# A compressed branch's first layer with high and low weights as one moving operand of 512 columns, and its parts added in the turn

## The reference

```python
blk = kr[:, idx] + pos[None, None, :, None, :]          # 31 windows of 32 tokens
flat = blk.transpose(0, 1, 3, 2, 4).reshape(B, nc, G, CMP_BLOCK * D)
return jax.nn.gelu(flat @ w1 + b1) @ w2                 # (62 x 2048) @ (2048 x 256)
```

## Time and profile before

| what | before |
|---|---|
| median of 3 runs | 1667.31 us (1667.16 to 1668.07) |
| profiled execution, its own time | 1668.98 us |
| its span | 1667.2 us |
| what lies around the span | 1.8 us |
| granted TensorE clock, mean | 0.996 of 2.4 GHz |
| TensorE busy | 1635.2 us, 98% |
| VectorE, ScalarE, GpSimd busy | 42%, 41%, 45% |

### The profile page before, as it was taken

How to read it: one execution, slowest core, us unless ns; L and a number is a source line. 1 busy time by engine, 2 the same in 40 slices (tenths; PEclk the granted TensorE clock), 3 DMA queues, 4 the chain that set the end, 5 groups by cost and what they waited for, 6 DMA issues and landing times.

```text
span 1667.2 us, 21229 instructions
## 1 busy us (share of the span) xinstructions
PE 1635.2 (98%) x8088; PEld 1349.0 (81%) x8088; DVE 692.5 (42%) x1395; ACT 684.6 (41%) x1204; POOL 753.7 (45%) x574
## 2 busy tenths in 40 slices
PE   9999999999999999999999999999999999999997
PEld 7777778888888887888888888888778888888885
DVE  6176664884444226312212225555673311112224
ACT  5366655543334324422223234566573422223322
POOL 7424325574445552744444553543113554444550
PEclk9999999999999999999999999999999999999999
DMA  5411102232232231323223222212002232222231
GB/s 202 146 51 51 39 14 101 102 101 91 99 102 90 99 101 51 123 93 101 97 92 101 95 96 101 89 65 77 26 26 89 89 101 95 95 101 92 98 101 51
DMA packets 42117, 147.37 MB, mean 88 GB/s; under 512 B 4768, under 2 KB 5152, under 8 KB 42016
## 3 DMA queue, kind: packets, MB, share of 16 engines
q1 hardware_dynamic: 40536, 143.13, 25.4%
q10 hardware_dynamic: 1480, 2.89, 0.5%
HBM read 142.84 MB, written 3.41 MB: 88 GB/s over the span
## 4 chain that ended last, share of the span: by engine, by line
PE 91%; DVE 3%; ACT 3%; issue 2%; DMA 1%; POOL 1%; DVEq 0%; ACTq 0%; POOLq 0%
PE PS L492 20%; PE PS L493 20%; PE PS L494 20%; PE PS L1059 5%; PE PS L1070 5%; PE PS L467 4%; PE PS L891 4%; PE PS L867 3%; PE PS L474 2%; PE PS L882 2%; PE PS L514 1%; PE PS L516 1%; PE PS L515 1%; DVE L L975 1%; POOL w_lo L536 0%
## 5 line engine op out<-in xcount | busy, mean ns | idle before, releaser
L536 POOL TENSOR_TENSOR w_lo<-stage,w_hi 128x512 fp32r<-128x512 f32 x524 | 709.5, 1379 | 843.5 <-ACT w_hi L524 842.5
L524 ACT ACTIVATE w_hi<-stage 128x1024 fp32r<-128x1024 f32 x262 | 274.7, 1057 | 509.1 <-DMA stage<-in_weights 508.9
L492 PE MATMUL PS<-H_hi,w_hi 128*128 128x512 f32 x992 | 387.7, 391 | 0.4 <-DVE rcol L1249 0.4
L494 PE MATMUL PS<-H_hi,w_lo 128*128 128x512 f32 x992 | 385.9, 389 | 0.0
L493 PE MATMUL PS<-H_lo,w_hi 128*128 128x512 f32 x992 | 385.9, 389 | 0.0
L492 PEld LDWEIGHTS PS<-H_hi,w_hi 128*128 128x128 f32 x992 | 186.2, 188 | 40.3 <-issue 1.0
L493 PEld LDWEIGHTS PS<-H_lo,w_hi 128*128 128x128 f32 x992 | 186.2, 188 | 39.5 <-issue 1.0
L494 PEld LDWEIGHTS PS<-H_hi,w_lo 128*128 128x128 f32 x992 | 186.2, 188 | 38.6
L492 PE MATMUL PS<-A_hi,w_hi 128*128 128x512 f32 x528 | 205.6, 389 | 0.3 <-DVE A_lo L646 0.2
L493 PE MATMUL PS<-A_lo,w_hi 128*128 128x512 f32 x528 | 205.4, 389 | 0.0
L494 PE MATMUL PS<-A_hi,w_lo 128*128 128x512 f32 x528 | 205.4, 389 | 0.0
(11 more groups left out here) (214 smaller groups left out, 2063.0 us busy)
## 6 DMA issues: line engine op xcount, KB each, us to landing
stage<-in_weights SPq DMA_DIRECT2D x262, 512.0 KB, 3.2
out_t<-Y SPq DMA_DIRECT2D x8, 256.0 KB, 2.0
X<-in_x_t SPq DMA_DIRECT2D x3, 512.0 KB, 8.3
bias_line<-bias_line ACTq DMA_DIRECT2D x1, 1270.0 KB
strip<-bias_line ACTq DMA_DIRECT2D x1, 1024.0 KB, 5.0
stage<-in_weights SPq DMA_DIRECT2D x2, 256.0 KB, 4.5
X<-in_x_t ACTq DMA_DIRECT2D x2, 256.0 KB, 6.0
V<-QF SPq DMA_DIRECT2D x4, 128.0 KB, 2.3
```

What stands on the lines that cost most here:

```text
L492: pe.matmul(out, a, h_hi, start=first, stop=False, skip_group_check=skip)
L494: return pe.matmul(out, b, h_hi, start=False, stop=last, skip_group_check=skip)
L524: act.activation(w_hi[:, slot, :], stage[:, slot, :], ACT.Copy).then_inc(hi_done, 1)
L536: lo = pool.tensor_tensor(w_lo[:, slot, cols], stage[:, slot, cols], w_hi[:, slot, cols].bitcast(F32), ALU.subtract)
```

## The change

The two weight buffers become one tensor, at the same addresses as before. For each k-step one matmul takes high and low weights side by side, 2 x 256 columns, and writes 512 columns of bank 7: product with the high weights left, with the low weights right. The third matmul (low data, high weights) stays at 256 columns. So there are two steps where there were three, 8 for a unit in place of 12. The two parts are added where the hidden layer is turned: each transpose becomes two accumulating float32 matmuls against the identity. The copies out of PSUM carry 512 columns in place of 256, and the values' one has another home, for which it waits on a DMA. The fill table is rewritten for the new step counts: the compressed layer's last step falls in item 39 (before 47), with all hooks counted from it; `kb` and `qb0` run at 3 steps an item over items 40 to 55 (before 6 steps an item over 48 to 51 and 53 to 56); the items without fill are 56, 65, 74 and 83 (before 52, 57, 66 and 75). The products with the values and their adds keep their items.

```diff
-FILL2 = [4] * 48 + [6] * 4 + [0] + [6] * 4 + [0] + [3] * 8 + [0] + [3] * 8 + [0] + [3] * 8
+FILL2 = [4] * 40 + [3] * 16 + [0] + [3] * 8 + [0] + [3] * 8 + [0] + [3] * 8 + [0]
 FILL2 = FILL2 + [(0, 4), 0] + [(0, 4), (3, 0)] * 5 + [(3, 12), (12, 6), 6]
...
-    return sum(12 if n in CMP_AT else 24 for n in FILL2_TASKS[:FILL2_TASKS.index(name) + 1])
+    return sum(8 if n in CMP_AT else 24 for n in FILL2_TASKS[:FILL2_TASKS.index(name) + 1])
...
-        w_hi = sb("w_hi", [P, RING, UNIT], F32R)
         with ExitStack() as scope:
 
+            sb("under", [P, RING, UNIT], ctx=scope)
             stage = sb("stage", [P, RING, UNIT], ctx=scope)
-        w_lo = sb("w_lo", [P, RING, UNIT], F32R)
+        w_both = sb("w_both", [P, 2, RING, UNIT], F32R)
+        w_hi, w_lo = w_both[:, 0, :, :], w_both[:, 1, :, :]
...
-            return QF[0:2 * NCMP, 0, s * CMP_HID:(s + 1) * CMP_HID]
+            return QF[0:2 * NCMP, s, :]
...
-            o = PS[0:2 * NCMP, 7, 0:CMP_HID]
+            o = PS[0:2 * NCMP, 7, :].rearrange("p (x c) -> p x c", x=2)
             for j4 in range(4):
                 j, cols = 4 * t + j4, slice(j4 * CMP_HID, (j4 + 1) * CMP_HID)
-                pe.matmul(o, kp_hi[:, j, :], w_hi[:, u % RING, cols], start=(j == 0), stop=False)
+                pe.matmul(o, kp_hi[:, j, :], w_both[:, :, u % RING, cols], start=(j == 0), stop=False)
                 yield
-                pe.matmul(o, kp_hi[:, j, :], w_lo[:, u % RING, cols], start=False, stop=False)
-                yield
-                mm = pe.matmul(o, kp_lo[:, j, :], w_hi[:, u % RING, cols], start=False, stop=(j == 15))
+                mm = pe.matmul(o[:, 0, :], kp_lo[:, j, :], w_hi[:, u % RING, cols], start=False, stop=(j == 15))
...
-                act.wait_ge(cm["raw"], 64)
+                act.wait_ge(cm["raw"], 64 * (s + 1))
                 wait_unit(act, fill2_unit(("cmp_k3", "cmp_v3")[s]))
-                act.activation(hidden(s), PS[0:2 * NCMP, 7, 0:CMP_HID], ACT.Copy).then_inc(cm["mlp"], 1)
+                act.activation(hidden(s), PS[0:2 * NCMP, 7, :], ACT.Copy).then_inc(cm["mlp"], 1)
...
-                    mm = pe.transpose(PS[:, 7, at:at + 2 * NCMP], hidden(s)[:, bass.ts(half, P)],
-                                      ident[0:2 * NCMP, 0:2 * NCMP])
+                    for part in range(2):
+                        mm = pe.matmul(PS[:, 7, at:at + 2 * NCMP], hidden(s)[:, bass.ts(2 * part + half, P)],
+                                       ident[0:2 * NCMP, 0:2 * NCMP], start=(part == 0), stop=(part == 1))
...
-            hook(at2, "pe", at + 18 + 2 * pair, pe_cmp_pv(pair))
-            hook(at2, "dve", at + 19 + 2 * pair, dve_cmp_add(pair))
+            hook(at2, "pe", at + 26 + 2 * pair, pe_cmp_pv(pair))
+            hook(at2, "dve", at + 27 + 2 * pair, dve_cmp_add(pair))
```

## The result

The changed kernel took 1673.11 us (median of 10 runs, 1671.28 to 1676.05), beside 1668.3 us for the kernel before on the same chip. The ratio is 1.0027, 95% interval 1.0018 to 1.0036: 4.5 us slower, within 3.0 to 6.0. Seven further runs in a later session gave 1672.52 us and 1.0029 (1.0018 to 1.0041). The forecast was +4.2 us, and 1671.5 us counted from a median before of 1667.31. A few of the timed executions, one of the kernel before at 3287 us among them, ran far slower and are left out of all ratios and intervals.

A forecast was written before the change was run, and what follows sets the result against it. TensorE, busy 98% of the span, was taken to bound the kernel. Terms +0.3 (fill), +1.4, +2.3, +0.7 and -0.5 summed to +4.2 us, 1671.5 us for the median; range 1667.0 to 1675.5.

The forecast's parts named there:

- fused steps in place: Compressed layer's fill on TensorE: 32 pairs of a 512 and a 256 replace 48 pairs of 256-column steps, -1.2 us.
- fill by the new table: TensorE's kb and qb0 fill, cut into 32 pieces in place of 16: more entries for as many columns, +1.5 us.
- turn: Hidden layer's turn on TensorE: eight float32 matmuls as 16 passes, 1.8 us, replace four transposes at 0.4: +1.4 us.
- series: VectorE's compressed softmax moves beside shorter items 50 to 55; TensorE waits 6.2 us where it waited 3.9: +2.3 us.
- evacuation: At item 48 qb0 begins on the bank kb just filled, so TensorE waits for VectorE to empty it: +0.7 us.
- windows: ScalarE's wait for GpSimd's windows moves from item 32 to 28; its 1.1 us on TensorE falls to 0.6: -0.5.
- gelu: ScalarE's gelu, now beside items of 384 keys: its work stays, 0 us, bounds -0.5 and +0.8.
- Rival 1: VectorE's series costs no more than before, or the float32 turn costs what transposes do: 1668.0 to 1669.2 us; chance 0.27.
- Rival 2: TensorE's time goes by instruction; 32 of 96 steps gone save 3.8 to 6.4 us: 1664.8 to 1667.4; chance 0.07.
- Rival 3: Faster: the softmax at items 50 to 55 is hidden altogether, -3.9 us, 1663.4; chance 0.12.
- Rival 4: Supply starves: each of 8 compressed units is late by 0.5, +4 us, 1675.5; chance 0.04.

The follow-up runs named there:

- second profile: The changed kernel, unaltered, profiled again: items 2 to 95 of the second block's attention (the stretch) 199.61 us against 195.65 before; timed ratio 1.0029.
- e1: Changed kernel's fused steps and turn, each in the item where the kernel before had them, hooks as before: ratio 1.0015 to the kernel before.
- e9: e7 with the fused steps in their old places and the two parts added by GpSimd, turn as four transposes: 1663.17 us, ratio 0.9971 to the kernel before.
- e11: Kernel before, without fusing and with four transposes, given the changed kernel's fill table by columns and its hooks: ratio 1.0017 to the kernel before.
- e4: Changed kernel with VectorE's four strip scalings hooked four items later, at item 39 in place of 35: ratio 1.0013 to the kernel before.
- e6: Changed kernel with the alterations of e3, e4 and e5, windows one item earlier and the compressed softmax cut smaller and spread: ratio 0.9978 to the kernel before.
- e2: Changed kernel with the hooks of the compressed branch eight items later, products in their items: ratio 1.0016 to the kernel before.
- e7: Kernel before with the compressed softmax cut smaller and spread over more items, and windows one item earlier: ratio 0.9961, again 0.997, to the kernel before.
- e3: Changed kernel with an item without fill between kb and qb0 (item 48) and none at item 83: ratio 1.0028 to the kernel before.
- e5: Changed kernel with GpSimd adding the two parts of the hidden layer, so the turn is four transposes again: ratio 1.0025 to the kernel before.
- e8: Changed kernel with 17 more float32 matmuls that nobody reads, in items 51 to 54 where TensorE waits: ratio 1.0019 to the kernel before.

## Why the prediction was right, and which of its steps were not

The verdict, slower by about 4, held. The sum held too: +4.2 forecast, +4.0 on the stretch of the second profile, +4.5 to +4.8 timed. In the second profile the low clock fell inside the waits; what it costs in the timed executions at large is open. But the sum is made of terms that are right, of two that are wrong and of one that was missing:

| term | forecast | measured | read from |
|---|---|---|---|
| fused steps in place | -1.2 | 0.0 to +0.1 | e1, e9 |
| fill by the new table | +1.5 | -1.6 | the remainder of e11 |
| turn | +1.4 | +1.5 | e1 item 49, e11 item 41 |
| series | +2.3 | +2.1 | below |
| evacuation | +0.7 | +0.6 | item 47 against 63 |
| windows | -0.5 | -0.5 | 0.7 of waits for 1.2 |
| gelu | 0 | +0.15 | items 43, 44: 1.6 for 1.44 |
| strips | not seen | +1.7 | e4 |
| sum | +4.2 | +4.0 | |

- **Turn.** Right, by the nearest row: 16 passes at 0.11. The bound at the price of transposes fell.
- **Series.** The mechanism and the size were right. Items 50 to 55 took 15.5 us (the changed kernel again; 16.6 said). Without waits, by items 50 and 51 themselves, items 52 and 54 of e6 and items 53 and 55 of e2 (this one with 0.36 for the turn that e2 has elsewhere), they would take 1.71 + 1.82 + 1.03 + 1.81 + 1.14 + 2.15 = 9.7 (10.4 said). With item 57's 0.3, an estimate, the waits are 6.2, as forecast; before, items 60, 61 and 63 lost 0.78 + 1.50 + 1.83 = 4.1 by the same items of e7 (3.9 said; for item 63 0.44 is taken off for the turn in it, which is what item 65 lost with its own). The first profile alone would have given 9 us and a false correction: 2.8 of it was clock.
- **Fill.** Here the working failed twice. I gave the fused stream -1.2 by comparing 32 pairs with 48. That gain belongs to the denser table and not to fusing: at the same density three short instructions cost 0.44 and two long ones 0.42. And I took the kernel before's fill items to be free of waits because the profile names none above 0.2 us. They weren't. Kernel before, item 21:

```profile
1094.53 0.36 PE L1115 MATMUL PS<-w_hi,kp_lo 128*62 128x256 f32 x1
1094.73 0.28 PE L1111 MATMUL PS<-w_hi,kp_hi 128*62 128x256 f32 x1
1095.08 0.41 PE L891 MATMUL PS<-V,tmp 128*128 128x64 f32 x2
```

The value product starts 0.35 behind the last step, where 0.12 is the pace: a delay of 0.23 that the row doesn't list as idle, by the very overlap of modelled ends that the prediction began with. With 512 columns more, item 21 went from 1.85 to 1.78 us (e11), where 0.23 more was due: the third step runs in the time that was lost. The same comparison of items 19, 21, 23, 37, 39, 41 and 57 (e4 for 37 and 39, e2 for 57, since there it has the same scores as before), each against its old length plus 0.23 for every 512 columns more (0.35 for 768 in item 39), and 0.4 for the turn in item 41, gives 0.11 + 0.30 + 0.36 + 0.31 + 0.30 + 0.52 + 0.48 = 2.4 us that the denser fill gave back. The remainder of the term, -1.6 + 2.4 = +0.8, is what more entries of `kb` and `qb0` cost; +1.5 was said. That last split is worked out, not tried by itself.
- **Strips.** The missing term. My own description says that hooks are counted from the fill, and I followed those of the compressed branch only. A VectorE step that took 0.9 us and was hidden in item 39 took 2.0 in item 35, beside a GpSimd subtraction, and cost TensorE 1.7.
- **Windows, evacuation, gelu.** Right within 0.2.
- **Rival 1** (turn at the price of transposes, or the series no dearer): both halves excluded. **Rival 2** (time goes by instruction): excluded by e1, e9 and e11. The sustained figure of the Trainium skill ("TensorE: Matmul & The Clock Gate", section "Back-to-back issue gap"), 131 ns for 512 columns, doesn't fit the 0.23 of the earlier trace rows. The formula that the same section gives for single, isolated matmuls, columns / 2.4 + 2.5 ns, comes to 216 ns for 512 columns and 109 for 256, as an estimate, and is near the 0.23 and 0.12 of the earlier trace rows. **Rival 3** (series hidden): no; but e7 shows that it can be hidden by spreading it. **Rival 4** (supply): no wait for weights stands in the items of the layer.

So the mechanism of the largest term, the series beside cheap items, was right, and the total was right partly by luck: a gain I hadn't seen (fill at -1.6 where +0.3 was forecast, 1.9 better) and a loss I hadn't seen (strips, +1.7) cancel.

## What to carry to other kernels

Where time goes by columns, as it did here, merging two matmuls with the same stationary operand into a wider one is worth next to nothing (at most 0.02 us a pair); what such an edit does is decided by the schedule it drags along. List *every* hook that is counted from the thing that changes length, on every engine, and for each ask beside which items it will stand: here a step of 0.9 us, moved among the shortest items and beside a GpSimd instruction, cost more (1.7 us) than the new arithmetic in the turn (1.5). And compare item by item by starts; the waits that a profile names are not all of them.

## What the runs showed of the hardware that I had not expected

- A VectorE scaling of 128 x 256 from SBUF to SBUF takes 0.29 us alone. In item 35 it took 1.37 when a GpSimd subtraction had started 0.08 us ahead of it (the changed kernel, both profiles, e2 and e11). In e4 one started beside it as well, and the subtraction took the longer time instead (2.70 us for the pair in place of 2.52).
- After waits of 0.5 to 2 us TensorE's granted clock went to 0.50 for 3 to 7 us in the profiles of the changed kernel, e3, e4, e5 and e11. Whether that cost 0 or 2.8 us depended on whether it fell inside the waits or behind them, and this differed between two executions of one kernel. Behind the waits of 0.55 to 1.58 us of the kernel before it stayed at 1.00.
- A float32 matmul of 128 x 62 against the identity is recorded as two passes of 0.11 us, a transpose of the same size as one, and four transposes cost about 0.4 in all where eight such matmuls cost 1.9 (e11 and the changed kernel, item 41: 1.53 apart).
- 17 spare float32 matmuls in the waits cost the stretch nothing (e8's 199.64 against 199.61).
